# Attention scores of a hybrid block: query parts stacked for the whole array, and the order of their preparation

## The reference

```python
q = rotary(rms_norm(q), positions)            # 16 heads of 64
k = rotary(rms_norm(k), positions)            # 4 heads of 64
s = einsum('bnqhgd,bnjhd->bhgnqj', qb, kwin) * 64 ** -0.5    # block of 128 queries, 3 blocks of keys
m = max(max(s), sink); p = exp(s - m)
p = p / (sum(p) + exp(sink - m))
o = einsum('bhgnqj,bnjhd->bnqhgd', p, vwin) * silu(gate)
```

## Time and profile before

| | |
|---|---|
| median of 3 runs | 2993.25 us (2993.08 to 2994.95) |
| the profiled execution, whole | 2995.79 us |
| the profiled execution, span from first to last instruction | 2994.0 us |
| mean granted TensorE clock | 0.997 of full speed |
| attention stage of layer 0, t = 0 to 23 | 588.8 to 690.4 us of the span, its last PV to 711.5 |
| attention stage of layer 1 | from 1578.3 us of the span |

### The profile page before, as it was taken

How to read it: one execution, slowest core, us unless ns; L and a number is a source line. 1 busy time by engine, 2 the same in 40 slices (tenths; PEclk the granted TensorE clock), 3 DMA queues, 4 the chain that set the end, 5 groups by cost and what they waited for, 6 DMA issues and landing times.

```text
span 2994.0 us, 41937 instructions
## 1 busy us (share of the span) xinstructions
PE 2962.3 (99%) x14220; PEld 2435.9 (81%) x14220; DVE 1746.1 (58%) x2633; ACT 1192.3 (40%) x1819; POOL 1412.7 (47%) x1040
## 2 busy tenths in 40 slices
PE   8999999999999999999999999999999999999998
PEld 6888888878888888888887888878888888788886
DVE  7986677874524598568687543367763344611214
ACT  4233333484333424333347533246554323422223
POOL 5443443455545443444355545534344544554544
PEclk9999999999999999999999999999999999999999
DMA  4222222212223322222221223222222323233222
GB/s 152 95 75 71 97 77 85 85 43 99 92 99 107 120 97 79 84 89 73 79 91 51 91 93 99 97 85 72 76 77 85 113 85 104 86 98 99 95 96 91
DMA packets 73273, 267.91 MB, mean 89 GB/s; under 512 B 8128, under 2 KB 9024, under 8 KB 72768
## 3 DMA queue, kind: packets, MB, share of 16 engines
q1 hardware_dynamic: 70560, 254.84, 25.6%
q10 hardware_dynamic: 2592, 11.46, 1.1%
HBM read 262.07 MB, written 4.19 MB: 89 GB/s over the span
## 4 chain that ended last, share of the span: by engine, by line
PE 86%; issue 7%; POOL 5%; ACT 1%; DVE 1%; DVEq 0%; ACTq 0%; POOLq 0%
PE gem L386 19%; PE gem L388 19%; PE gem L387 19%; POOL wlo L319 5%; PE gem L800 2%; PE gem L802 2%; PE gem L801 2%; PE gem L508 2%; PE gem L509 2%; PE gem L507 2%; PE gem L627 2%; PE gem L629 1%; PE gem L628 1%; PE gem L653 1%; PE xp L671 1%
## 5 line engine op out<-in xcount | busy, mean ns | idle before, releaser
L319 POOL TENSOR_TENSOR wlo<-raw,whi 128x512 fp32r<-128x512 f32 x956 | 1317.9, 1400 | 1548.6 <-ACT whi L962 1548.5
L962 ACT ACTIVATE whi<-raw 128x1024 fp32r<-128x1024 f32 x478 | 504.3, 1056 | 671.1 <-PE gem L388 514.5
L386 PE MATMUL gem<-zhi,whi 128*128 128x512 f32 x1664 | 649.5, 390 | 0.3 <-DVE zlo L1609 0.3
L388 PE MATMUL gem<-zhi,wlo 128*128 128x512 f32 x1664 | 647.6, 389 | 0.0
L387 PE MATMUL gem<-zlo,whi 128*128 128x512 f32 x1664 | 647.4, 389 | 0.0
L386 PE MATMUL gem<-hhi,whi 128*128 128x512 f32 x1280 | 498.7, 390 | 0.0
L388 PE MATMUL gem<-hhi,wlo 128*128 128x512 f32 x1280 | 498.0, 389 | 0.0
L387 PE MATMUL gem<-hlo,whi 128*128 128x512 f32 x1280 | 498.0, 389 | 0.0
L386 PEld LDWEIGHTS gem<-zhi,whi 128*128 128x128 f32 x1664 | 312.4, 188 | 65.5 <-DVE zlo L1609 0.8
L388 PEld LDWEIGHTS gem<-zhi,wlo 128*128 128x128 f32 x1664 | 312.4, 188 | 65.4
L387 PEld LDWEIGHTS gem<-zlo,whi 128*128 128x128 f32 x1664 | 312.4, 188 | 64.7 <-issue 0.2
(11 more groups left out here) (439 smaller groups left out, 4346.0 us busy)
## 6 DMA issues: line engine op xcount, KB each, us to landing
raw<-in_slabs SPq DMA_DIRECT2D x478, 512.0 KB, 3.4
U<-in_x SPq DMA_DIRECT2D x4, 512.0 KB, 7.2
U<-in_x ACTq DMA_DIRECT2D x1, 2048.0 KB, 10.0
xsave<-U ACTq DMA_DIRECT2D x1, 2048.0 KB, 6.5
U<-xsave ACTq DMA_DIRECT2D x1, 2048.0 KB, 9.9
out_y<-yr SPq DMA_DIRECT2D x8, 256.0 KB, 2.2
tab<-in_tab_ret ACTq DMA_DIRECT2D x2, 512.0 KB, 7.9
tab<-in_tab_att ACTq DMA_DIRECT2D x2, 512.0 KB, 3.6
```

Of the source, the lines that this page charges most:

```text
L319: part = pool.tensor_tensor(wlo[:, k % 4, c], raw[:, k % 2, c], whi[:, k % 4, c].bitcast(f32), O.subtract)
L386: pe.matmul(o, wh, hi, start=(n == 0), stop=False)
L388: mm = pe.matmul(o, wl, hi, start=False, stop=(n == len(terms) - 1))
L962: act.activation(whi[:, k % 4, :], raw[:, k % 2, :], A.Copy).then_inc(hi_done, 1)
```

## The change

The query parts are laid out anew. Where a pair had one tile of high parts and one of low parts, each head now has a tile: its high part on its own half of the partitions and its low part on the other half. A key head's high part is copied to both halves, and its low part stands on the query's high half with zeros on the other half. One matmul of the whole array, 128 channels deep, then gives high by high and low by high; the second gives high by low. So a block has two matmuls for each head, all of 128 rows, where it had three of 64 rows.

The keys' tiles are now one per key head. Those of heads 0 and 1 stand where both key pairs stood; those of heads 2 and 3 overlay the raw query tiles 0 to 3 and are made in the stretch: high parts on ACT at t = 4 and 7 (after a wait for the low parts of query pairs 0 to 3), fill with zeros and low part on DVE at t = 7 and 10. ACT's high parts of the query pairs 4 to 7 move from t = 5, 8, 11, 14 to t = 3, 6, 9, 15, DVE's low part of pair 7 from t = 15 to 18, and the steps of the last rotation from t = 4, 7, 10, 13 to t = 5, 8, 11, 14, where they come after the gate and the split.

```diff
--- before.py
+++ after.py
@@ -192,13 +192,19 @@
         LB, OML, NBF, LBT = lbs[:, 0:8], lbs[:, 8:16], lbs[:, 16:24], lbs[:, 24:40]
 
 
-        def key_parts(L, pr):
-
-            return tuple(t[:, 6 + pr, :] for t in Z[L])
+        def key_parts(L, i):
+
+            if i < 2:
+                return tuple(t[:, 6 + i, :] for t in Z[L])
+            return tuple(Ur[:, a + (i - 2) * T:a + (i - 1) * T] for a in (U_A + 2 * T, U_C))
 
         def query_parts(L, p):
 
             return tuple(t[:, (p + 4) % 6, :] for t in Z[L])
+
+        def head_rows(hf):
+
+            return slice(hf * 64, hf * 64 + 64), slice(64 - hf * 64, 128 - hf * 64)
 
         def mean_parts(n):
 
@@ -635,7 +641,7 @@
                     p, c = t // 3, t % 3
                     pr = p // 4
                     pe.wait_ge(x_ready, L * 8 + p + 1)
-                    pe.wait_ge(k_ready, L * 2 + pr + 1)
+                    pe.wait_ge(k_ready, L * 4 + 2 * pr + 2)
                     if t == 0:
                         pe.wait_ge(evac[0], u + 1 + PRIMED)
                         pe.wait_ge(evac[1], u + 1 + PRIMED)
@@ -644,14 +650,13 @@
                         pe.wait_ge(vt_ready, L * 2 + 2)
                     else:
                         pe.wait_ge(p_exp, L * 24 + (t - 1))
-                    (qh, ql), (kh, kl) = query_parts(L, p), key_parts(L, pr)
                     for n, cols in spans(c):
                         lo, hi = max(n - 1, 0), min(n + 2, 4)
-                        for q, key, first, last in ((qh, kh, True, False), (ql, kh, False, False), (qh, kl, False, True)):
-                            for hf in range(2):
-                                d = slice(hf * 64, hf * 64 + 64)
-                                mm = pe.matmul(scores_of(t, hf)[:, cols], q[d, n * P:(n + 1) * P],
-                                               key[d, lo * P:hi * P], start=first, stop=last)
+                        for hf in range(2):
+                            o, x = scores_of(t, hf)[:, cols], query_parts(L, p)[hf][:, n * P:(n + 1) * P]
+                            kh, kl = key_parts(L, 2 * pr + hf)
+                            pe.matmul(o, x, kh[:, lo * P:hi * P], start=True, stop=False)
+                            mm = pe.matmul(o, x, kl[:, lo * P:hi * P], start=False, stop=True)
                     mm.then_inc(s_done, 1)
 
                 def turn_p(t):
@@ -1215,15 +1220,19 @@
                     a_inv(k - 1)
                     a_square(k)
 
-                def keys_high(pr):
-
-                    act.wait_ge(a_rope, L * 10 + pr + 1)
-                    act.activation(key_parts(L, pr)[0], KA[:, pr, :], A.Copy).then_inc(k_high, 1)
+                def keys_high(i):
+
+                    src, kh = KA[head_rows(i % 2)[0], i // 2, :], key_parts(L, i)[0]
+                    act.activation(kh[0:64, :], src, A.Copy)
+                    act.activation(kh[64:P, :], src, A.Copy).then_inc(k_high, 1)
 
                 def queries_high(p):
 
                     act.wait_ge(a_rope, L * 10 + 3 + p)
-                    act.activation(query_parts(L, p)[0], QR[p], A.Copy).then_inc(x_high, 1)
+                    for hf in range(2):
+                        r = head_rows(hf)[0]
+                        last = act.activation(query_parts(L, p)[hf][r, :], QR[p][r, :], A.Copy)
+                    last.then_inc(x_high, 1)
 
                 high(G + 3, 3)
                 for k in range(3):
@@ -1232,6 +1241,7 @@
                     if k < 2:
                         a_square(k + 4)
                     if k == 0:
+                        act.wait_ge(a_rope, L * 10 + 1)
                         keys_high(0)
                         keys_high(1)
                     else:
@@ -1291,8 +1301,11 @@
                         act.activation(TH, gem[:, 3, :], A.Tanh, scale=0.5).then_inc(th_ready, 1)
                     if t < 24:
                         exps(t)
-                    if t in (5, 8, 11, 14):
-                        queries_high(p + 3)
+                    if t in (4, 7):
+                        act.wait_ge(x_ready, L * 8 + 4)
+                        keys_high(p + 1)
+                    if t in (3, 6, 9, 15):
+                        queries_high(7 if t == 15 else p + 3)
                     if t % 3 == 1 and t < 24:
                         high(G, 4 + p + 3)
                     if t in (22, 23):
@@ -2014,17 +2027,22 @@
                         key_low(1)
                     a_rotated(n)
 
-                def keys_low(pr):
-
-                    kh, kl = key_parts(L, pr)
-                    dve.wait_ge(k_high, L * 2 + pr + 1)
-                    tt(kl, KA[:, pr, :], kh.bitcast(f32), O.subtract).then_inc(k_ready, 1)
+                def keys_low(i):
+
+                    r, other = head_rows(i % 2)
+                    kh, kl = key_parts(L, i)
+                    dve.wait_ge(k_high, L * 4 + i + 1)
+                    dve.memset(kl[other, :].bitcast(f32), 0.0)
+                    tt(kl[r, :], KA[r, i // 2, :], kh[r, :].bitcast(f32), O.subtract).then_inc(k_ready, 1)
 
                 def queries_low(p):
 
-                    qh, ql = query_parts(L, p)
                     dve.wait_ge(x_high, L * 8 + p + 1)
-                    tt(ql, QR[p], qh.bitcast(f32), O.subtract).then_inc(x_ready, 1)
+                    for hf in range(2):
+                        r, other = head_rows(hf)
+                        x = query_parts(L, p)[hf]
+                        last = tt(x[other, :], QR[p][r, :], x[r, :].bitcast(f32), O.subtract)
+                    last.then_inc(x_ready, 1)
 
                 for k in range(4):
                     a_rotated(k + 2)
@@ -2109,16 +2127,18 @@
                     p, c = t // 3, t % 3
                     maxes(t)
                     normalise(t - 1)
+                    if t in (7, 10):
+                        keys_low(p)
                     if c == 2:
                         gate(p)
                     if c == 0 and p >= 2:
                         gated_head(p - 2)
-                    if t in (3, 6, 9, 12, 15):
-                        queries_low(p + 2)
+                    if t in (3, 6, 9, 12, 18):
+                        queries_low(7 if t == 18 else p + 2)
                     if c == 2 and p >= 2:
                         head_split(p - 2)
-                    if t in (4, 7, 10, 13):
-                        turn_step(9, t // 3 - 1)
+                    if t in (5, 8, 11, 14):
+                        turn_step(9, p - 1)
                 normalise(23)
                 gated_head(6)
                 dve.drain()
```

## The result

| | before | after |
|---|---|---|
| median of 5 runs | 2993.78 us (2993.08 to 2994.95) | 3007.02 us (3005.78 to 3008.75) |
| span of the profiled execution | 2994.0 us | 3005.5 us |

The ratio is 1.0043 [1.0031, 1.0054]: slower by 13 us, where 3 were forecast and the range ended at 3001. The profiled executions differ by 11.5 us.

What follows compares the result with a forecast made beforehand. PE was taken to bound the kernel, busy 2962 of 2994 us, with ACT and DVE nearly full. PE's 7.3 us saving was lost to waits at PV, leaving 3.1 us slower: 2996.3 us, range 2987 to 3001.

Steps and rivals of the forecast that it cites:

- main case: Whole kernel: PE's 7.3 us saving is stood out at PV, 3.1 us slower over two layers, 2996.3 us; chance 0.60.
- PE's own terms: Score groups on PE: new matmul steps and removed seams save 3.65 us a layer, 7.3 us in all.
- the first stall: PV at t = 6: PE waits 1.7 us for ACT's copies and passes 0.59 us later than before.
- the seams: Either end of a score group on PE: exposed weight loads, expected to go except the 0.09 exit seam before PV.
- Rival B: Score groups: the change does not remove the seam, PE pays 9.3 us more, 3002.6 us; chance 0.08.
- An inserted one costs 0.53.: ACT: each inserted copy of 64 rows costs 0.53 us, bounds 0.27 and 0.62.
- It starts 0.58 earlier: ACT ahead of PV at t = 6: work starts 0.58 us earlier, as PE ends slab 4 sooner.
- less the idle 0.83: ACT from t = 9 on: its idle 0.83 us, and 0.17 ahead of the third copy, are deducted from the lateness.
- A DVE low part ... I take 0.6 inserted: DVE: an inserted low part of 64 rows costs 0.6 us; half of 0.68 is the lower bound, at worst 1.78.
- After t = 18: End of the stretch: nothing inserted on ACT, PE's lateness shrinks by 0.42 and 0.46, from 2.43 to 1.55 us.
- A: Rival: side engines have room, copies of 64 rows cost half (0.27 us); 2987.2 us, with no stall 2985.9; chance 0.18.
- C: Rival: DVE's new work is dear, two low parts of a period 1.1 us dearer while POOL subtracts; 3003.3 us; chance 0.14.

Runs made afterwards that it cites:

- the products alone: Kernel before with only its score matmuls replaced by two whole-array matmuls per head on the old tiles, no side work added: 2987.96 us.
- Experiment 6: Kernel after, but DVE makes one low part of 128 rows for each of query pairs 3 to 7; ACT keeps two copies: 3004.56 us.
- half the stacking: Stacked form for query pairs 0 to 3 only; pairs 4 to 7 and key heads 2 and 3 keep the old 64-row pairs: 2991.25 us.
- experiment 3: Kernel after with the last rotation's steps moved back to t = 4, 7, 10, 13: 3004.3 us.
- experiment 10: Kernel after with second halves of late query and key work (copies, query low parts, key fills) on POOL, ACT/DVE work later, rotation back: 3000.43 us.

## Why the prediction was wrong

It was wrong in size: the sign of the main case held, and its time was 10.7 us short. PE's own terms and the first stall were near; what the side engines' work costs from period to period was not.

- **PE's terms held.** Steps 0.118 and 0.173 were forecast, 0.119 and 0.17 to 0.18 came, and the seams are gone. Of 7.3 us, 6.2 showed in the products alone. That weight loads of the whole array are hidden also holds, against the rule on row groups of the Trainium skill that the prediction cites: a step of 0.119 has no room for an exposed load of 0.19. Rival B falls.
- **"An inserted one costs 0.53."** Each cost 0.64, since copies of 64 rows did not overlap their neighbours in ACT's queue. Four at the first PV are 0.44 more.
- **"It starts 0.58 earlier"** (the exponentials of t = 3). They start at 607.29, before 608.38: 1.09 earlier, of which 0.90 is the program's start, so 0.19. DVE had only 0.27 us idle ahead of that gate. The gate came 0.43 earlier by the same reckoning (604.18 for 605.51), and a small operation behind it (L2066, now L2084) took 0.52 for 0.29. So the copies ahead of the first PV were 1.48 late by the clock of the trace, and 2.38 against PE's start, where 1.54 stood.
- **The first stall, 1.7, came out at 1.73, partly by luck.** PE passed 1.49 late against its start and not 0.59, but it had lost some of its advance already: score groups from t = 5 on waited for exponentials and low parts (the row of L658 in the waits). I had not priced that wait.
- **The rotation step at t = 5 was left out.** I counted it at t = 8, 11 and 14, but it also stands behind the first gate, 0.99 us, ahead of the maxima of t = 6. Those exponentials came 0.89 late (620.37 to 621.26), where PE's lateness explains 0.57.
- **The failed step: "less the idle 0.83" and "less 0.17", from t = 9 on.** In each period I let ACT's idle time swallow what was late, and charged DVE only with the rotation, 0.85. "A DVE low part ... I take 0.6 inserted" came out at 0.96 to 1.1, and the rotation and the slower split at 1.07 behind the gate. That is 2.0 us a period on DVE for the 1.32 of idle time in the earlier trace rows. So from t = 11 DVE was the busy engine, and ACT's idle time was no longer a reserve but a wait for DVE: 1.72 and 0.94 us at t = 12 and 13. The period from t = 12 to 15 shows it best: 0.15 to be won back, 0.93 lost. From t = 6 to 18 the forecast added 1.84 us a layer and the run 4.67.
- **After t = 18** I gave PE back 0.88. It got back 0.25.
- **The clock was not in the sum.** In the profile it cost 1.25 us, once, in layer 1.
- **Rivals.** A fell at the first row of ACT: half the rows cost the full time. C had the engine and the sign right. Its reason was a low part dearer by 1.1 us while POOL subtracts, twice a layer. In the stretch the second low part of every pair was dearer by 0.3 instead; whether POOL is behind that is open (see the end). Experiment 6 shows that DVE's low parts alone are worth 2.5 us, so C's pure form is too narrow as well: it takes both engines.

## What to carry to other kernels

When two engines feed each other once in a period, don't treat the idle time of each as a reserve of its own. Follow the ring once around with all inserted work, and see which engine's wait the idle time turns into. Before half-height operations are put on the side engines, price one in its place: here half the rows saved nothing. And a gain on the bounding engine (6 us here) is worth only as many inserted side operations as the ring has idle time for: half the stacking kept 3 us, the whole lost 13.

## What the runs showed of the hardware beyond that

- ACT's copy of 64 rows by 512 columns took 0.62 to 0.63 us, like 128 rows. Copies of 64 rows started 0.64 apart, copies of 128 rows followed at 0.53.
- DVE's subtraction of 64 rows took, in the stretch, 0.68 to 0.69 for the first head and 0.98 for the second, at all five pairs of layer 0. What makes the second dearer stays open. POOL scaled probabilities beside all five of them, and where POOL stood idle (567.93 and 574.76) the second took 0.69; but the first took 0.69 beside POOL too, and so did one second in experiment 3 (1617.67).
- A fill of 64 rows by 512 took DVE 0.48 and POOL 0.52 us. POOL's subtraction of 64 rows took 1.26 to 1.55.
- TensorE's clock did not answer to the length of a stall alone. Behind the same stall of 1.73 us it stayed at 1.00 in layer 0 of the kernel after and fell to 0.50 (1.2 GHz) in layer 1, which cost 1.25 us. It also fell behind the first stall of layer 0 in experiments 3 and 6 (1.72 and 1.73 us), and not in layer 1 of either.
- Behind the stall of 2.89 us in experiment 10 it was down for some 7 us, in which 40 products took 4.49 us where 2.40 is usual. By the runs of experiment 10 (2995.27 us at a mean clock of 0.998, 3003.14 at 0.995) the falls of both layers cost up to 7.9 us, more than the 5.8 us of the two standstills themselves.
